# Loading the first adaLN weights in shift/scale pairs between the first products, and splitting the sums of squares over two engines

## The reference

```python
def rms_norm(x, g):
    y = x * rsqrt(mean(x * x, axis=-1) + EPS)
    return y * g

def modulate(x, g, shift, scale):
    return rms_norm(x, g) * (1.0 + scale) + shift

# per layer: six chunks of 1024 from silu(c) @ ada_w + ada_b: shift and scale of norm 1 come first
h   = modulate(x, norm1_g, shift, scale)       # latent tokens with c, context tokens with c_ctx
p   = h @ w_in                                 # combined input projection; pooling columns among them
# attention, gated delta net and pooling heads on p, output projection, gated residual,
# then a second modulated norm and an expert-choice mixture of 16 experts, gated residual
```

## Time and profile before

| what | us |
|---|---|
| median of 3 runs | 1903.32 |
| lowest, highest run | 1902.9, 1905.24 |
| span of the profiled execution, first to last instruction | 1899.8 |
| the runs above that span (1902.9 to 1905.24 less 1899.8), which is what lies around it | 3.1 to 5.4 |
| first product of layer 0 (L636) starts at | 48.25 |
| first product of layer 1 (L636) starts at | 1095.27 |

### The profile page before, as it was taken

The page is one execution under the profiler, slowest core; times in us unless marked ns, Lnnn a source line. Parts: engine busy times, 40 slices in busy tenths (PEclk is TensorE's granted clock), DMA queues, the critical chain, the costliest instruction groups (busy, mean ns, idle before and its releaser), DMA issues.

```text
span 1899.8 us, 40923 instructions
## 1 busy us (share of the span) xinstructions
PE 1787.0 (94%) x17297; PEld 1101.5 (58%) x17297; DVE 720.6 (38%) x1447; ACT 482.4 (25%) x1074; POOL 420.4 (22%) x542
## 2 busy tenths in 40 slices
PE   6999999989999998999999999999888899899998
PEld 4565555667777544665556445555577764545554
DVE  3145333455553234111111525334466633432323
ACT  3311442353323132101101231253433222100010
POOL 1603100146662002211111032200267720100000
PEclk7999999999999998999999999999999999999999
DMA  9420000076556216899998412000300022599996
GB/s 324 140 69 22 1 23 1 3 239 194 185 184 227 67 45 256 307 365 367 365 359 318 135 45 67 22 1 1 101 14 25 14 97 104 194 409 413 408 413 240
DMA packets 140855, 321.24 MB, mean 169 GB/s; under 512 B 11208, under 2 KB 98894, under 8 KB 125358
## 3 DMA queue, kind: packets, MB, share of 16 engines
q1 hardware_dynamic: 127584, 287.20, 40.7%
q0 software_dynamic: 6432, 20.00, 3.8%
q10 hardware_dynamic: 6702, 12.05, 2.1%
HBM read 305.77 MB, written 13.45 MB: 168 GB/s over the span
## 4 chain that ended last, share of the span: by engine, by line
PE 83%; DVE 7%; ACT 3%; issue 3%; DMA 2%; SPq 1%; POOL 0%; ACTq 0%; DVEq 0%; POOLq 0%
PE psum L636 17%; PE psum L1174 11%; PE psum L1074 7%; PE psum L1205 6%; PE psum L756 3%; PE psum L1183 3%; PE psum L1255 3%; PE psum L943 3%; PE psum L561 2%; PE psum L777 2%; PE psum L925 2%; PE psum L1217 2%; PE psum L859 1%; PE psum L809 1%; PE psum L983 1%
## 5 line engine op out<-in xcount | busy, mean ns | idle before, releaser
L636 PE MATMUL psum<-hT,ring 128*128 128x256 f32 (+2 forms) x976 | 337.2, 503 | 4.2 <-ACT hT L1578 3.8
L636 PEld LDWEIGHTS psum<-hT,ring 128*128 128x128 f32 (+1 forms) x976 | 184.6, 192 | 144.5 <-issue 127.2
L1174 PE MATMUL psum<-ring,arena 128*64 128x256 f32 x1536 | 175.7, 386 | 5.8 <-DVE xT L2492 3.6
L1174 PEld LDWEIGHTS psum<-ring,arena 128*64 128x64 f32 x1536 | 109.9, 139 | 68.7 <-issue 14.4
L1074 PE MATMUL psum<-hT,ring 128*128 128x512 f32 (+1 forms) x384 | 139.4, 522 | 0.9 <-DVE xT L2376 0.9
L2463 DVE TENSOR_TENSOR arena<-arena,psum 128x384 f32<-128x384 f32 (+1 forms) x32 | 15.6, 488 | 260.0 <-PE psum L1183 160.8
L1074 PEld LDWEIGHTS psum<-hT,ring 128*128 128x128 f32 x384 | 72.9, 190 | 64.6 <-issue 61.4
L1849 ACT COPY ring<-psum 128x256 f32<-128x256 f32 x240 | 72.5, 384 | 124.3 <-PE psum L943 123.1
L943 PE MATMUL psum<-wbuf,ring 64*64 64x64 f32 x1920 | 76.8, 228 | 26.0 <-DVE wbuf L2340 18.4
L2798 POOL DMA_INDIRECT big<-h_rows_lat,idx x16 | 15.6, 977 | 382.8 <-PE psum L1279 174.8
L2340 DVE TENSOR_TENSOR wbuf<-lev,psum 128x256 f32<-128x256 f32 x120 | 45.1, 417 | 135.5 <-PE psum L925 135.5
(11 more groups left out here) (352 smaller groups left out, 3303.9 us busy)
## 6 DMA issues: line engine op xcount, KB each, us to landing
ring<-in_moe_w_gate SPq DMA_DIRECT2D x64, 1024.0 KB, 10.3
ring<-in_ada_w SPq DMA_DIRECT2D x48, 1024.0 KB, 5.9
ring<-in_moe_w_up SPq DMA_DIRECT2D x32, 1024.0 KB, 9.9
hT<-in_moe_w_down SPq DMA_DIRECT2D x24, 1024.0 KB, 10.7
ring<-in_w_in SPq DMA_DIRECT2D x20, 1024.0 KB, 7.0
big<-in_moe_w_up SPq DMA_DIRECT2D x16, 1024.0 KB, 10.6
sz<-in_moe_w_down SPq DMA_DIRECT2D x16, 1024.0 KB, 8.5
big<-in_moe_w_down SPq DMA_DIRECT2D x16, 1024.0 KB, 14.4
```

The lines of the kernel that those rows point to most:

```text
L636: m = pe.matmul(b[0:c1 - c0, 0:n], lhsT=w[:, k, c0:c1], rhs=hT[:, k, t0:t0 + n], start=k == 0, stop=k == KD - 1)
L1174: m = pe.matmul(b[e * CAP_L:(e + 1) * CAP_L, 0:2 * P], lhsT=xs[:, k, e, 0:CAP_L], rhs=w[e][:, 2 * (k - ks[0]) + q, :], start=k == 0, stop= ...
```

## The change

The first eight adaLN loads change their order and their place. They come as pairs, shift and scale of the same two blocks: columns 0 and 4 (of 256 each), 1 and 5, 2 and 6, 3 and 7. TensorE does the first pair and its columns ahead of the sum over the partitions, the second pair behind it, and the third and fourth pair between the products of `pool0` and `pool1`, which now share one loop over the blocks. All column products of these loads stand by themselves in a bank of their own ("am"), and VectorE makes the modulation of two blocks at a time (`first_modulation`); ScalarE copies the rows from inside its `norm`.

The sums of squares of the first norm of both layers are split: VectorE adds the latent columns (512), GpSimd the context columns (256). At the joint, squares and adds go in the order `halves`, inside the loop of the last pair's residual updates. ScalarE's table load for Ln and Exp moves ahead of the squares in layer 0. The warm-up products stay.

The loads' order and TensorE:

```diff
-ADA_ALL = [(l, g) for l in range(DEPTH) for g in range(ADA_LOADS)]
+ADA_PAIRS = ADA_FIRST // 2
+ADA_ALL = [(0, g) for q in range(ADA_PAIRS) for g in (q, ADA_PAIRS + q)]
+ADA_ALL += [(l, g) for l in range(DEPTH) for g in range(ADA_LOADS) if l or g >= ADA_FIRST]
...
-            return a == 0 or ADA_FIRST <= a <= ADA_LATE
+            return a <= ADA_LATE
...
                 pe.wait_ge(s[sqd], KD)
                 done(pe.matmul(lat, lhsT=ones[:, :], rhs=sqsum[:, CTX:T], start=True, stop=True), ("ss", l, which, 1))
+                if which == 1:
+                    pe.wait_ge(s["sqp1"], KD)
...
+            def first_loads(q):
+                for a in (2 * q, 2 * q + 1):
+                    ada_load(0)
+                    ada_load(1)
+
+            def first_columns(q):
+                key = ("am", q)
+                b = claim(key)
+                for n in range(2):
+                    m = ada_columns(2 * q + n, b[:, 4 * n:4 * n + 4])
+                done(m, key)
...
                     evacuated(pe, "c")
-                    for a in range(SLOTS):
-                        if a == 1:
-                            pe.wait_ge(s_sum, 16)
-                        ada_load(0)
-                        ada_load(1)
+                    first_loads(0)
+                    pe.wait_ge(s_sum, 16)
+                    first_columns(0)
                 sum_over_partitions(l, 1, "sq1", "sqd1")
                 if l == 0:
-                    for a in range(SLOTS, ADA_FIRST):
-                        ada_load(0)
-                        ada_load(1)
-                    ada_last(ADA_FIRST - 1)
+                    first_loads(1)
+                    first_columns(1)
...
                 w = weights(("in", l, 0))
-                chunk(("in", l, "pool0"), w, 0, P, segs)
-                chunk(("in", l, "pool1"), w, P, 2 * P, segs)
+                pools = [(c, g, claim(("in", l, "pool%d" % c, g))) for c in range(2) for g in segs]
+                held.extend(where[("in", l, "pool%d" % c, g)][0] for c, g, _ in pools)
                 last_use(None, ("in", l, "pool1", 1))
+                for k in range(KD):
+                    pe.wait_ge(s["h1"], k + 1)
+                    for c, g, b in pools:
+                        t0, n = SEGS[g]
+                        m = pe.matmul(b[:, 0:n], lhsT=w[:, k, c * P:(c + 1) * P], rhs=hT[:, k, t0:t0 + n],
+                                      start=k == 0, stop=k == KD - 1)
+                        if k == KD - 1:
+                            done(m, ("in", l, "pool%d" % c, g))
+                    if l == 0 and k in (1, 3):
+                        first_loads(2 + k // 2)
+                    if l == 0 and k in (2, 4):
+                        first_columns(1 + k // 2)
```

ScalarE:

```diff
+                if n >= 2:
+                    act.wait_ge(s["sqd%d" % which], n - 1)
+                    if which == 1:
+                        act.wait_ge(s["sqp1"], n - 1)
+                act.activation(sqb[:, n % 2, t0:T], xT[:, k, t0:T], ACT.Square).then_inc(s["sq%d" % which], 1)
...
+                by_pair = which == 1 and l == 0
                 for k in range(KD):
+                    if by_pair and k in (0, 4, 6):
+                        for a in range(2):
+                            ada_out(max(k, 2) + a)
+                    act.wait_ge(s["mods%d" % which], k // 2 + 1 if by_pair else 1)
                     act.wait_ge(s["hx%d" % which], k + 1)
...
-                if k:
+                if k == 0:
+                    act.preload_act_table_set(LOG_EXP)
+                else:
                     first_squares(k - 1)
+            first_squares(KD - 1)
             ada_out(0)
-            first_squares(KD - 1)
-            for a in range(1, SLOTS):
-                ada_out(a)
+            ada_out(1)
```

VectorE:

```diff
+                if which == 1:
+                    t0 = CTX
...
+            def first_modulation(q):
+                key = ("am", q)
+                b = product_ready(dve, key)[:, 0:8].rearrange("p (n m c) -> p n m c", n=2, m=2)
+                for n in range(2):
+                    m0 = n * KD + 2 * q
+                    m = dve.tensor_tensor(modraw[:, m0:m0 + 2, :], b[:, n, :, :],
+                                          cols[:, m0:m0 + 2].unsqueeze(2).to_broadcast([P, 2, 2]), ALU.add)
+                read_out(m, key)
+                evacuated(dve, key)
+                dve.scalar_tensor_tensor(
+                    out=amod_of[0][:, 0, 2 * q:2 * q + 2, :], in0=modraw[:, KD + 2 * q:KD + 2 * q + 2, :], scalar=1.0,
+                    in1=cols[:, COL_N1 + 2 * q:COL_N1 + 2 * q + 2].unsqueeze(2).to_broadcast([P, 2, 2]), op0=ALU.add,
+                    op1=ALU.mult).then_inc(sems[0]["mods1"], 1)
...
-                    modulation(0, 0)
-                    norm(l, 1)
+                    first_modulation(0)
+                    norm(l, 1, range(2))
+                    first_modulation(1)
+                    norm(l, 1, range(2, KD))
+                    first_modulation(2)
+                    first_modulation(3)
...
+                        if not nxt and l + 1 < DEPTH and halves.index(k) >= 2:
+                            add_squares(l + 1, 1, halves.index(k) - 1)
+                    if not nxt and l + 1 < DEPTH:
+                        add_squares(l + 1, 1, KD - 1)
```

GpSimd:

```diff
+                for n in range(1, KD):
+                    pool.wait_ge(s["sq1"], n + 1)
+                    if n >= 2:
+                        pool.wait_ge(s["sqp1"], n)
+                    before = sqsum if n >= 2 else sqb[:, 0, :]
+                    pool.tensor_tensor(sqsum[:, 0:CTX], before[:, 0:CTX], sqb[:, n % 2, 0:CTX], ALU.add
+                                       ).then_inc(s["sqp1"], 2 if n == 1 else 1)
...
-                    evacuated(pool, ("am", ADA_FIRST - 1))
+                    evacuated(pool, ("am", ADA_PAIRS - 1))
                     parameters(0)
```

More of the change, by code:

```diff
@@ L341, in build_program @@
         s_out = sem("s_out")
[L342 removed]
+        NAMES = ["zero", "pcol", "par", "mods1", "mods2", "rinv", "sq1", "sqd1", "hx1", "h1", "sqp1", "sq2", "sqd2", "hx2", "h2", "upad", "pool", "sqm",
                  "abw", "abraw", "abexp", "abln", "gbd", "row1", "rowr", "rowa", "row2", "nm", "rden", "cv1", "qkv", "lsq",
@@ L394, in scores_ready @@
             b = where[("s", l, i, h)][0]
-            return psum[:, b:b + 2, :].rearrange("p a c -> p (a c)")[:, 0:(CT if i < CT else NT) * P]
+            if i < CT:
+                return psum[:, b, 0:CT * P]
+            return psum[:, b:b + 2, :].rearrange("p a c -> p (a c)")[:, 0:NT * P]
         def attended(eng, l, calls, n):
@@ L653, in _ @@
                 w = weights(("in", l, 0))
-                chunk(("in", l, "pool0"), w, 0, P, segs)
-                chunk(("in", l, "pool1"), w, P, 2 * P, segs)
+                pools = [(c, g, claim(("in", l, "pool%d" % c, g))) for c in range(2) for g in segs]
+                held.extend(where[("in", l, "pool%d" % c, g)][0] for c, g, _ in pools)
                 last_use(None, ("in", l, "pool1", 1))
+                for k in range(KD):
[10 more added lines that the diff above has]
+                        first_columns(1 + k // 2)
+                for c, g, _ in pools:
+                    held.remove(where[("in", l, "pool%d" % c, g)][0])
                 w = weights(("in", l, 1))
@@ L1501, in _, with squares @@
             act.dma_start(iota[:, :], A["k_iota"]).then_inc(s_sum, 16)
-            def squares(l, which, k):
+            def squares(l, which, k, n=None):
                 s = sems[l]
+                n = k if n is None else n
                 t0 = 0 if which == 1 or l == 0 else CTX
-                if k >= 2:
-                    act.wait_ge(s["sqd%d" % which], k - 1)
-                act.activation(sqb[:, k % 2, t0:T], xT[:, k, t0:T], ACT.Square).then_inc(s["sq%d" % which], 1)
+                if n >= 2:
[3 more added lines that the diff above has]
+                act.activation(sqb[:, n % 2, t0:T], xT[:, k, t0:T], ACT.Square).then_inc(s["sq%d" % which], 1)
             def inverse_roots(l, dst, keys, bias, scale):
@@ L1621, in _ @@
                 t_first = tiles[0] * P
-                act.preload_act_table_set(LOG_EXP)
                 if l:
-                    for k in range(KD):
+                    act.preload_act_table_set(LOG_EXP)
+                    for n, k in enumerate(halves):
                         for g in (0, 1):
                             evacuated(act, ("last", l - 1, "c%d%d" % (k, g)))
-                        squares(l, 1, k)
+                        squares(l, 1, k, n)
                 norm(l, 1)
@@ L1907, in _ @@
                 hw = 3 * P if need_ctx else 2 * P
+                halves = [k for q in range(KD // 2) for k in (q, q + KD // 2)]
                 def tokens(name_of, i, q):
@@ L2017, in _ @@
                 t_first = i0 * P
-                for k in range(1 if l else KD - 2, KD):
-                    add_squares(l, 1, k)
+                if l == 0:
```

(12 more changed lines are left out.)

14 lines of the change are left out of this document (3 added, 11 removed).

## The result

| kernel | median | lowest to highest | runs | profiled execution, its span |
|---|---|---|---|---|
| before | 1904.28 | 1902.9 to 1907.33 | 4 | span 1899.8 |
| after | 1888.32 | 1886.77 to 1890.28 | 4 | 1886.77, span 1885.0 |

The ratio after/before is 0.9913 [0.9897, 0.9928], about 16.6 us faster (16.0 by the medians). Three things to read in the trace: the start, the joint, and one place that the sum had put at nothing.

What follows compares the result with a forecast made beforehand. TensorE's instruction order was taken to bound the kernel (83% of the chain). Gains of 7.3 at the start and 4.0 at the joint sum to 11.3: span 1899.8 to 1888.5, median 1892.0, range 1888.5 to 1898.

Steps and rivals of the forecast that it cites:

- one place that the sum had put at nothing: Layer 0's attention: waits that the turn of PSUM banks could move, taken as 0.
- The bound and the places: Whole kernel: TensorE's instruction order bounds it (83% of the chain); the change touches the start and the joint.
- I charge the same 1.9 again: Layer 0's pool products: 1.9 us lost at the low clock, as in the kernel before.
- I take 0, bound 1 each way: PSUM banks after the pool products: later claims turn by one bank, effect 0, bound 1 us each way.
- Squares, 1.3 less: Layer 0's start: narrower VectorE adds end the last square 1.3 us earlier, at about 24.9 instead of 26.17.
- squares late: Rival, layer 0's start: VectorE and GpSimd take adds in turn, costing 3.6, time 1895.6; chance 0.08.
- The start up to the pool products: Layer 0: first pool product at about 34.8, 13.4 us earlier than 48.25.
- clock stays low longer: Rival, layer 0's start: clock doesn't rise before the first pool product, 3.6 in all, time 1895.6; chance 0.14.
- The table load: Layer 0's start: ScalarE's Ln/Exp load moved behind its first copy makes copy 1 0.4 late; cost 0, bound 0.4.
- No stall in the pool stage, transfers 0: Layer 0's pool products: no block comes late, margin 0.6 only; moved weight and parameter transfers cost 0 each.
- The joint, 4.0: Joint of the layers: sum starts 1.8 earlier and the shared pool loop gains 2.2, together 4.0.
- The warm-up products bind: Joint: 16 warm-up products still stand ahead of the sum, so it gains 1.8, not 5.5.

Runs made afterwards that it cites:

- e11: Kernel after, with layer 0's first pool product waiting for three modulated blocks instead of one; 1896.63, ratio 0.9959 to the kernel before.
- e8: Kernel after once more, unchanged, for a second profile and more times; 1891.38, ratio 0.9922 to the kernel before.
- e3: Kernel after with the third and fourth adaLN pair ahead of the pool products, not between them; 1891.99, ratio 0.9951 to the kernel before.
- e6: Kernel after with layer 1's two pool chunks one after the other again; 1890.44, ratio 0.9932 to the kernel before.
- e1: Kernel before with only the joint changed (squares and adds reordered, adds split, layer 1's pool chunks in one loop); 1899.86, ratio 0.9974.
- e4: Kernel after with 3 instead of 8 warm-up products ahead of the sum at the joint; 1882.74, ratio 0.9893 to the kernel before.
- e10: Kernel after with one PSUM bank skipped behind layer 0's pool products, restoring the earlier banks; 1891.52, ratio 0.9934 to the kernel before.
- e5: Kernel after with four unused products filling TensorE's gap before the first columns; 1887.93, ratio 0.9912 to the kernel before.
- e12: Kernel after with both 3 instead of 8 warm-up products at the joint and four filling products at the start; 1883.12, ratio 0.989 to the kernel before.
- e9: Kernel before with seven PSUM banks skipped behind layer 0's pool products, giving the banks of the kernel after; 1902.26, ratio 0.9993.
- e7: Kernel before once more, unchanged, for a second profile; 1904.74, ratio 0.9994 to the kernel before.

## Why the prediction was right or wrong

*The bound and the places: right.* TensorE's order is 84% of the chain after too, and everything that changed stands at the start, at the joint and in one bank wait.

*"I charge the same 1.9 again": wrong, and the larger of two failed terms.* The reason given was that TensorE has only column products between 32.9 and 34.8, "as at 44 to 48 us". The likeness was the wrong one. In 45 to 51 us TensorE was busy 2.88 of 6.00; in 31 to 34 us of the kernel after it was busy 2.23 of 3.00, with a gap of 0.95. e11 restores a long gap and with it 2.35 of loss; the short gap cost nothing in seven of eight profiles, so that the loss stayed away is what a gap of this length mostly gives, with a share of luck. Without the term the sum is 34.8 + 20.64 + 4.0 + 2.2 = 61.6, a gain of 9.2 at the start; measured were 9.9 and 8.9.

*Banks, "I take 0, bound 1 each way": wrong.* It was 1.9. The turn by one bank was seen; what was not done is to ask of each wait in the earlier trace rows which claim it hung on. The longest, 1.7, was a claim that began at the bank of the product before it, because of where banks happened to be passed over; with the turn they are passed over elsewhere. The bound of 1 had no row behind it; the row's own 1.7 was the least to allow for.

*Squares, 1.3 less: the mechanism of the bound came, its price didn't.* The last square ends at 25.80 instead of 26.17, not 24.9. VectorE's adds do take 0.68. But VectorE's and GpSimd's adds don't run at once, as the sum had it: where GpSimd's began behind VectorE's (17.77 behind 17.70), it takes 0.99 to 1.24 instead of 0.72 and ends 0.58 to 0.60 after VectorE's, in all 17 such pairs of the two profiles of the kernel after, four of them at the joint. Where GpSimd's began alone it takes 0.72 to 0.73, and VectorE's add that began inside it (1064.45, GpSimd's from 1064.21 to 1064.94) takes 1.03. Whoever comes second waits for the first. The Trainium skill (GPSIMD Engine Reference, Key points) warned of contention when VectorE's instruction has two SBUF inputs. The trace agrees, and on both engines: VectorE's copies out of PSUM stay at 0.68 beside GpSimd's adds.

So the full turn-taking that I kept as the bound, and as the rival "squares late", did happen. It cost 0.9 against the forecast 24.9, not 3.6. The bound put each add's 1.40 against 0.68, but between two adds VectorE also copies a block, another 0.68, and GpSimd's remaining 0.6 lies under that copy. From 21.37 on the squares follow one another at 1.20, the pace of VectorE's add and copy, which start 0.60 apart; in the kernel before it was 1.47. GpSimd's share shows only where ScalarE waits for it (1.24 ahead of 19.09, 0.36 ahead of 24.96). TensorE's sum starts at 27.29, forecast 27.2, because the later columns (26.21 instead of 25.2) take 1.22 for both sets, not 2.02; that was the clock of this execution, and in e8 they take 1.84 and the sum starts at 27.95.

*The start up to the pool products: right.* 34.18 and 34.93 against 34.8. Loads 2 and 3 took 1.99 in the one profile, 1.0 each, where one was charged at half clock: that is the 0.6, and the second profile hasn't got it. The rival "clock stays low longer" didn't occur.

*The table load: right.* The next copy starts at 15.47 instead of 15.17 and the first square 0.3 later with it, but the second is level again (16.74 and 16.72).

*No stall in the pool stage, transfers 0: right.* From 38 to 60 us TensorE is busy 22.00 of 22.00. GpSimd's parameter transfers went out 8 us later and its pooling started at 61.19 (61.30 before, forecast 65), with nothing behind it late. e3 shows the other side: with the pool weights ninth again, the first product waits 0.75 for them.

*The joint, 4.0: right.* 1.8 by the sum (measured 1.86), 2.2 by the merged loop (e6: 2.2), together 4.24 in e1 and 4.25 in the kernel after. The warm-up products bind, as said, and e4 shows their price.

*The sum with the measured terms:* 9.9 (8.9) + 1.9 + 4.25 = 16.0 (15.0), against 16.0 by the medians of the result and 13.4 by that of e8 and its session's kernel before (ratios: 16.6 and 14.9). What is left, 1 to 2 us each way, is no more than what two profiles of one kernel drift apart in code that nobody changed (0.8 to 4.7 in the kernel after). It can't be assigned further from these runs.

## What to carry to other kernels

In these traces the half-clock loss behind a place went with the idle time ahead of it, not with the kind of product that stands there: find the gap that the changed order will have before charging the loss again, and give a short gap a chance of the loss rather than the loss. When claims of a rotating resource move by one, follow each existing wait to the claim that it hangs on; its own length is the first size to put on what the turn can give or take, and a low clock behind it can add to that (e10). And when an edit removes a wait that filler work was sized for, size the filler anew in the same change: here that was some 4 us more for one constant.

## What the runs showed of the hardware

- VectorE's 128x512 and GpSimd's 128x256 fp32 add, each with two SBUF inputs, take turns. The one that starts second ends 0.55 to 0.62 after the first: GpSimd's takes up to 1.24 instead of 0.72 to 0.73, VectorE's up to 1.24 instead of 0.68 (at 17.73 in e8; 1.03 at the joint of the kernel after). VectorE's 128x512 copy from PSUM stays at 0.68 to 0.69 beside them.
- Eight instructions of unused products in TensorE's 3.8 us gap keep the granted clock at 1.00 from 23 to 34 us (e5), where it is 0.72 and 0.62 without them. The mark moves by 1.4, or 2.2 against e8; in the times no gain is shown, and in e12 the clock falls all the same 3 us after the filled stretch.
- The same instructions in the same order can differ by 3.5 us within the first 70 us. ScalarE's first read of `pool1` in the four profiles of the old start came at 67.87 (e9), 69.82 (e7), 70.00 and 71.39 (e1). TensorE's first column product already differs by 0.9 (24.14 in e9, 25.02 in the kernel before); the rest goes with when the clock rises. A claim about 1 us needs the trace at the place, and more than one of them.
